# The last stage of a one-core PEER layer: groups of six expert tiles instead of four, with the sums taken in two halves

## The reference

```python
def block(args):
    xk, ik, gk = args
    act = jax.nn.gelu(jnp.einsum('tkd,td->tk', expert_u[ik], xk))
    return jnp.einsum('tk,tkd->td', gk * act, expert_v[ik])
...
x = x + peer_ffn(rmsnorm(x, norm2), peer_wq, peer_keys, peer_u, peer_v)
y_prompt = rmsnorm(xp, final_norm)
```

## Time and profile before

| what | value |
|---|---|
| median of 3 executions | 3219.15 us (3218.26 to 3221.4) |
| the profiled execution's own time | 3221.37 us |
| its span | 3219.6 us |
| mean granted TensorE clock | 0.987 of full speed |
| busy share of the span: PE, DVE, POOL | 97%, 80%, 35% |
| the last stage | from 2150 us to the end, a third of the span |
| HBM traffic | 233 GB/s over the span |

### The profile page before, as it was taken

One profiled execution on the slowest core, in us unless ns is written; L12 is line 12 of the kernel. 1 busy time (PEld: TensorE's weight loads), 2 busy tenths in 40 slices (PEclk: granted clock), 3 DMA queues, 4 the chain that ended last, 5 costly groups with the idle time before them and its releaser, 6 DMA issues. The chain is left out here.

```text
span 3219.6 us, 45871 instructions
## 1 busy us (share of the span) xinstructions
PE 3107.1 (97%) x17420; PEld 2726.2 (85%) x17420; DVE 2569.2 (80%) x5687; ACT 883.4 (27%) x1307; POOL 1126.0 (35%) x758
## 2 busy tenths in 40 slices
PE   8999989899999999999999999998999999999998
PEld 7867765499999999999999999987777777777776
DVE  6621244357799999989888988858999999999996
ACT  4210300132122222224444444422222222222222
POOL 0000000000032222223333333324555886688881
PEclk9999989999999999999999999999999999999999
DMA  3010021351187777768888889899999999999993
GB/s 103 15 41 29 14 88 51 99 163 55 49 264 246 246 243 245 243 209 287 294 286 325 288 292 325 285 331 339 343 344 343 336 347 350 339 344 346 347 347 138
DMA packets 359908, 754.88 MB, mean 234 GB/s; under 512 B 37085, under 2 KB 205881, under 8 KB 354041
## 3 DMA queue, kind: packets, MB, share of 16 engines
q0 software_dynamic: 102576, 373.47, 34.3%
q1 hardware_dynamic: 257112, 378.49, 34.0%
HBM read 647.21 MB, written 102.25 MB: 233 GB/s over the span
## 5 line engine op out<-in xcount | busy, mean ns | idle before, releaser
L1931 POOL DMA_INDIRECT lead<-in_peer_v_dram,chosen x212 | 424.2, 2001 | 179.1 <-DVE acc_s L1950 128.1
L1931 POOL DMA_INDIRECT gr_row<-in_peer_u_dram,chosen x205 | 229.8, 1121 | 462.0 <-DVE chosen L1940 454.5
L1907 ACT ACTIVATE up_a<-up_pa 128x352 f32<-128x352 f32 x256 | 118.9, 464 | 755.3 <-PE up_pa L1892 662.5
L1931 POOL DMA_INDIRECT dr_row<-in_peer_v_dram,chosen x140 | 282.6, 2019 | 99.9 <-DVE acc_s L1950 72.4
L2694 DVE TENSOR_TENSOR acc<-pd_po,acc 128x512 f32<-128x512 f32 x384 | 278.7, 726 | 25.5 <-PE pd_po L2761 22.6
L1931 POOL DMA_INDIRECT s_sb<-in_peer_u_dram,chosen x147 | 159.3, 1084 | 374.7 <-DVE chosen L1940 369.1
L1950 DVE SCALAR_TENSOR_TENSOR acc_s<-lead,chosen,acc_s 128x1024 f32<-128x1024 f32 x212 | 279.9, 1320 | 0.0
L2340 ACT ACTIVATE lo_wx<-room 128x704 fp32r<-128x704 f32 x128 | 101.6, 794 | 623.6 <-DVE room L2331 623.6
L1940 DVE CUSTOM_DVE_ANT_0 gr_row<-gr_row,xs 128x1024 f32<-128x1024 f32 x205 | 248.6, 1220 | 14.4 <-DMA gr_row<-in_peer_u_dram,chosen 14.4
L511 PE MATMUL fr_a<-pj_w,h_t 128*128 128x256 f32 (+1 forms) x864 | 199.3, 393 | 0.9 <-PEq L186 0.9
L2462 DVE TENSOR_SCALAR pg_hot_i<-pg_iota,sel_t 128x128 f32<-128x128 f32 x704 | 195.7, 358 | 0.0
(11 more groups left out here) (484 smaller groups left out, 7420.1 us busy)
## 6 DMA issues: line engine op xcount, KB each, us to landing
lead<-in_peer_u_dram SPq DMA_DIRECT2D x128, 512.0 KB
room<-in_peer_v_dram SPq DMA_DIRECT2D x128, 512.0 KB
act_d<-up_a SPq DMA_DIRECT2D x256, 176.0 KB
room<-w_d SPq DMA_DIRECT2D x64, 704.0 KB, 6.6
room<-act_d SPq DMA_DIRECT2D x64, 704.0 KB
w_d<-pg_wb SPq DMA_DIRECT2D x24, 1024.0 KB, 7.0
w_d<-room SPq DMA_DIRECT2D x20, 1024.0 KB
lead<-in_peer_wq_dram SPq DMA_DIRECT2D x20, 512.0 KB, 3.9
```

The lines of the kernel that those rows point to most:

```text
L1907: self.nc.scalar.activation(self.a_sb[c][:], self.pa[c][:, 0:WB], ACT.Gelu_apprx_tanh).then_inc(self.a_act, 1)
L1931: pool.indirect_dma_start(self.buf[i % self.n], None, self.table, bass.IndirectOffsetOnAxis(ap=self.idx[:, col:col + 1], axis=0)).then_inc ...
```

## The change

Groups of six tiles (`GE = 6`), the last of eight: `NG = 21`. The operands of eight tiles are one ring (`RING = 8`): tile m is written where tile m - 8 was, as soon as PE has used that tile for the last time (`freed`). PE makes a group's sums in two halves of six sums, and inside a half goes tile by tile over six PSUM banks at once. The two banks of the fold join the others, so eight go round (`NBANKS`), one half of the sums in six of them while two more are free. DVE's order is written anew in ticks (one tile of one half, 17 matmuls): 240 ticks and the last group's. The operands are made eight ticks ahead, by `made_by`. The rows are spread by `ROOM_AT` over the six ticks of a half: one, then two in each of four, then none. The additions of a half's sums stand together: four at the end of its last tick, two at the start of the next. Some loads of `acc` are issued later at the start, and slots leave in another order at the end.

```diff
-GE = 4
+GE = 6
+RING = 8
...
-        self.nc.scalar.activation(self.vx[m // GE % 2][m % GE][0], self.v[m % 2], ACT.Copy).then_inc(self.v_hi, 1)
+        self.nc.scalar.activation(self.vx[m % RING][0], self.v[m % 2], ACT.Copy).then_inc(self.v_hi, 1)
...
+SIZES = (GE,) * 20 + (NK - 20 * GE,)
+NG = len(SIZES)
 OUTS = 2 * ND
+HALF_OUTS = OUTS // 2
...
-FIRST_ROW = 12
-ROWS_EARLY = 18
...
+TICKS = 2 * GE * (NG - 1)
+AHEAD = 8
+ROWS_FROM, ROWS_TO = 6, TICKS - 4
+ROOM_AT = (1, 2, 2, 2, 2, 0)
+
+FINAL = (6, 7, 0, 1, 8, 2, 5, 3, 4)
...
+def made_by(tick):
+
+    return min(3 * NK, 3 * (tick + AHEAD) // 2 + max(0, 3 * (tick - TICKS + 6) // 2))
...
-                g, e = m // GE, m % GE
-                if e == 0 and g >= 2:
-                    act.wait_ge(o_done, OUTS * (g - 1))
+                if m >= RING:
+                    g, e = (m - RING) // GE, (m - RING) % GE
+                    if e < GE - 1:
+                        act.wait_ge(freed, (GE - 1) * g + e + 1)
+                    else:
+                        act.wait_ge(filled, sum_at(g, OUTS - 1) + 1)
...
-            for g in range(NG):
-                for o in range(OUTS):
-                    m = GE * (g + 1) + o // 3
-                    if g == 0:
-                        add(g, o)
-                    if m < NK:
-                        (lower.multiply, lower.low_v, lower.low_w)[o % 3](dve, m)
-                    if g >= 1:
-                        add(g, o)
-                    at = OUTS * g + o - FIRST_ROW
-                    for i in range(rows_by(at), rows_by(at + 1)):
...
+            for tick in range(TICKS + SIZES[-1]):
+                last = tick >= TICKS
+                g = NG - 1 if last else tick // (2 * GE)
+                half, e = (0, tick - TICKS) if last else divmod(tick % (2 * GE), GE)
+                if e == 0 and tick >= GE:
+                    for o in (HALF_OUTS - 2, HALF_OUTS - 1):
+                        add(g if half else g - 1, o + (0 if half else HALF_OUTS))
+                make(made_by(tick), made_by(tick + 1))
+                for i in range(rows_by(tick), rows_by(tick + 1)):
+                    if i == 0:
+                        dve.wait_ge(accs_in, 16 * NXS)
+                    rows_v.add(dve, i, gate, acc_s)
+                if e == SIZES[g] - 1:
+                    for o in range(HALF_OUTS - 2):
+                        add(g, HALF_OUTS * half + o)
...
+            def half_sums(g, half):
+                for e in range(SIZES[g]):
+                    m = GE * g + e
+                    if half == 0:
+                        pe.wait_ge(v_lo, m + 1)
+                        pe.wait_ge(w_lo, m + 1)
+                    for o in range(HALF_OUTS * half, HALF_OUTS * (half + 1)):
+                        if e == 0:
+                            bank_free(sum_at(g, o))
                         mm = product(g, o, e)
-                    mm.then_inc(o_done, 1)
+                        if e == SIZES[g] - 1:
+                            mm.then_inc(filled, 1)
+                    if half == 1 and e < SIZES[g] - 1:
+                        mm.then_inc(freed, 1)
```

More of the change, by code:

```diff
@@ new lines, in _ @@
+            g = NG - 1
+            inverse(0)
+            add(g, HALF_OUTS - 2)
+            inverse(1)
+            add(g, HALF_OUTS - 1)
+            take(FOLD_REST, x_s)
+            dve.wait_ge(gain_loaded, 16)
+            weigh(0)
+            inverse(2)
+            weigh(1)
+            add(g, HALF_OUTS)
+            inverse(3)
+            weigh(2)
+            add(g, HALF_OUTS + 1)
+            inverse(4)
+            weigh(3)
+            take(FOLD_HALF, acc[0:HALF_P, ND - 1, :])
+            inverse(5)
@@ L2755, in _ @@
+            weigh(4)
+            add(g, HALF_OUTS + 2)
+            inverse(6)
+            weigh(5)
+            add(g, HALF_OUTS + 3)
+            inverse(7)
+            weigh(6)
+            add(g, HALF_OUTS + 4)
+            weigh(7)
+            add(g, HALF_OUTS + 5)
+            inverse(8)
+            weigh(8)
         @block.tensor
@@ L2760, in product @@
                 for x, y in parts:
-                    mm = nc.tensor.matmul(po[(OUTS * g + o) % NPO][:], lower.tokens(wx[g % 2][e], s, y),
-                                          vx[g % 2][e][x][:, half * W4:(half + 1) * W4],
-                                          start=(e == 0 and (x, y) == parts[0]), stop=(e == GE - 1 and (x, y) == parts[-1]))
-                return mm
-            for e in range(GE):
-                pe.wait_ge(v_lo, e + 1)
-                pe.wait_ge(w_lo, e + 1)
-                for o in range(NPO):
-                    mm = product(0, o, e)
-                    if e == GE - 1:
-                        mm.then_inc(o_done, 1)
@@ new lines, in product, with bank_free @@
+                    mm = nc.tensor.matmul(banks[sum_at(g, o) % NBANKS][:], lower.tokens(wx[m % RING], s, y),
+                                          vx[m % RING][x][:, half * W4:(half + 1) * W4],
+                                          start=(e == 0 and (x, y) == parts[0]), stop=(e == SIZES[g] - 1 and (x, y) == parts[-1]))
+                return mm
+            def bank_free(at):
+                if at == NBANKS - 1:
+                    pe.wait_ge(up.a_act, 2 * NK)
+                if at >= NBANKS:
+                    pe.wait_ge(emptied, at - NBANKS + 1)
@@ new lines, in _ @@
+            for g in range(NG - 1):
+                for half in range(2):
+                    half_sums(g, half)
+            half_sums(NG - 1, 0)
+            pe.wait_ge(shaped, PACKED)
+            pe.wait_ge(rows_v.used, COLS)
+            fold_into(FOLD_REST, LAST, [(fold[i], acc_s[:, NSP + i, :]) for i in range(len(PACKS))])
+            for o in range(HALF_OUTS, OUTS):
+                if sum_at(NG - 1, o) == FOLD_HALF + 2:
+                    pe.wait_ge(emptied, BASE + 2)
+                    fold_into(FOLD_HALF, HALF_P, [(fold[0][:, 0:HALF_P], acc[:, ND - 1, :])])
+                bank_free(sum_at(NG - 1, o))
+                for e in range(SIZES[-1]):
+                    mm = product(NG - 1, o, e)
+                mm.then_inc(filled, 1)
```

144 lines of the change are left out of this document (57 added, 87 removed).

## The result

| kernel | median | runs | ratio to before, 95% interval |
|---|---|---|---|
| before | 3220.28 us | 4 (3218.26 to 3221.79) | |
| changed | 3247.99 us | 4 (3244.54 to 3252.86) | 1.0084 (1.0072 to 1.0097) |

The changed kernel is slower, by 28 us. I had forecast 102 us. Its profiled execution took 3246.93 us, its span is 3245.2.

A forecast was written before the change was run, and what follows sets the result against it. DVE bounds the stage. Its 12 ticks were put at 47.3 us plus 7.5 of row waits, D = 54.8; 2290.0 + 18.83 x D gave 3322 us, 3.2% slower, with an 8-in-10 range of 3212 to 3363.

The forecast's parts named there:

- the term for the port: Middle stage: POOL's fetches are held during DVE's two-operand SBUF work, so DVE waits 7.5 us for rows in 12 ticks.
- With that boundary open: If fetches can leave between an operand step and a row, DVE's row waits are 6.5, 7.9 and 6.4 us.
- Seven openings for 9.2 rows: Per half, three fetches leave during additions, four before pairs' second rows; two leave only because DVE has run dry.
- a fetch of 2901.42: Fetch in the kernel before, started during a row and ending 0.81 us after the low part behind it.
- The third rival: Part of the port's cost: step-into-row openings open, landings short, waits 2.1 to 5 us, 3220 to 3275 us; chance 16%.
- 47.3 us without waits: DVE's 12 ticks in the stage: additions, rows and operands 45.97 us plus 1.3 for second rows of pairs.
- D: Time of 12 ticks in the stage, forecast as 47.3 + 7.5 = 54.8 us.
- PE's pace: PE's matmuls in the stage at 0.2288 us each, 204 in 12 ticks: 46.7 us, nothing added for bank changes.
- The sum: Whole execution: 2290.0 + 18.83 x D, from the span of 3219.6 us; 3322 us with D at 54.8.
- PE runs free to its last sum: After tick 236 DVE has no rows, so PE is unhindered to the stage's end; 1.5 us less there.
- The loads bound: Rival: loads of 17.1 MB in 12 ticks take 48.5 us, 3203 us; 4%, within the 14% for an uncounted port.
- Signs: Expected profile: DVE idle 6 to 9 us per 12 ticks for rows, PE waiting about 4 us each half.

The follow-up runs named there:

- e2: Changed kernel with six row buffers in place of five, two packed acc_s slots merged into one and one small start load left out: 3208.69 us, ratio 0.9958.
- e3: Changed kernel with each row fetch bringing 256 KB, half the bytes, with as many descriptors: 3201.36 us, ratio 0.9939.
- e10: Changed kernel with rows brought by plain loads that SP issues through the hardware queue, POOL fetching nothing in this stage: 3202.34 us, ratio 0.9936.
- e7: Changed kernel with sparse columns reordered so a pair's two rows belong to two acc_s slots and the second doesn't wait: 3259.91 us, ratio 1.012.
- e5: Like e1 (operand steps and rows one by one), plus one VectorE wait per half behind the last addition of the run: 3174.84 us, ratio 0.9848.
- e9: Kernel before, with POOL's row transfers as plain DMAs of 128 neighbouring rows instead of indirect ones: 3224.16 us, one execution.
- e6: Kernel before, with one VectorE wait in each group of 12 sums, for the addition just issued: 3227.72 us, ratio 1.0017.
- e1: Changed kernel with VectorE's operand steps and rows one by one in each half, so rows no longer pair: 3204.43 us, ratio 0.9936.
- e4: Changed kernel with both steps and rows one by one and six row buffers: 3207.95 us, ratio 0.9951.

## Why the prediction was right or wrong

**The step that failed** is the term for the port: "With that boundary open the waits are 6.5, 7.9 and 6.4. The mean of the six is 7.5", and under it "Seven openings for 9.2 rows". It measured 2.8 us in 12 ticks. I took a fetch of 2901.42, held across row and low part, as the rule for that boundary. It belonged to a run of late fetches, in a stretch in which VectorE hadn't waited for 670 us. The changed kernel waits in every pair, and behind a row that VectorE has waited for, the boundary to the next step let out every fetch that asked, 111 of 111. I had counted the gap inside the pair as an opening, but not the one that it makes behind the pair. The third rival, "Openings that I count as shut (operand step into row) are open", gave 3220 to 3275 us for 16%, and holds 3248, but not by its own account: it named the boundary from a step into a row, where 37 fetches left, not that from a row to a step, and it counted on short landings, and these are not short: 6.35 us above, where I had stepped through 3.6, 4.5 and 5.5. That my range of 3212 to 3363 holds the time is luck as well. It reached down to the break-even, and its middle rests on the port. The 2.8 us of waits that are left come from five buffers against a trip of fetch and landing, as e2, e3 and e10 show; the port is in it with part of the fetch, and a port more shut makes them larger (68.2 us in 800 in e7).

**The other terms**, at their word:
- *47.3 us without waits* (45.97 and 1.3 for pairs). D less row waits is 50.2 - 2.8 = 47.4 in the changed kernel, 47.6 in e3 and e10 (47.8 less 0.2). Right. The pair: 2.67 us for two rows, thus 1.39 from start to start in place of 1.19, 0.20 for my 0.16.
- *PE's pace.* 0.2288 a matmul was 1% high: e5 makes 3,510 in 797 us, 0.2271. The more frequent bank changes cost nothing that shows.
- *Start.* Tile 8's multiply began at 2195.9, forecast 2195.5.
- *The sum.* 2290.0 + 18.83 x 50.2 = 3235.3 for a span of 3245.2. The 10 us that lack stand behind tick 234. PE waited 5.2 us for the last group's banks, since VectorE had waited for the loads of the last tiles (2.7 and 2.3 us), and its clock fell:

```profile
3137.00:3165.00 28.00, 25.93 (x106) 0.94 0.86 308
3165.00:3175.00 10.00, 5.40 (x15) 0.66 0.05 19
```

A share of 0.94 in 28 us is 1.7 us of full speed, 0.66 in 10 us is 3.4, part of it in the wait itself. "PE runs free to its last sum" was wrong by this much, and the clock that I left out is some of it.
- *The loads bound.* I gave 360 GB/s at a share of 1; e5 moved 366 at 0.99. By that the loads didn't bind even at 46.5 us in 12 ticks.
- *Signs.* Waits on `lead` and `dr_row`, PE's wait at the third sum: right. The sizes were too large: 28 waits of PE, 44.3 us together, for the 31 halves in 800 us, and 4.1 the longest, where I had put 4 in each. Fetches of 1 to 1.7 us amid rows and low parts, which I had named as the sign against the port step, were there (2722.29 and 2724.28).

The Trainium skill (SBUF — State Buffer, section "Who interferes with whom") infers that tensor_tensor doesn't delay a DMA, since descriptor making needs only the write side. By e9 that holds for a plain DMA that POOL issues, 0.53 us each; it doesn't for an indirect one, of which 197 took 2.29 us and more in before.

**Where the gain went.** The change takes 79 us of additions from VectorE, and without waits D would have been 46.5 to 47.4: faster than before, as e5 shows. It was given back by two rows to a tick with five buffers (45.0 us of waits in the middle, where before had none), by the pairs (160 x 0.20 = 32 us of VectorE's time), and by 10 us at the end.

## What to carry to other kernels

A measured stall has a condition. Before pricing it a hundred times over, look at what the engine did ahead of that one case, and at cases where it didn't happen: the 2.62 us of 2901.42 needed a row that VectorE hadn't waited for. A number that comes out as a theory said (e6) doesn't show the theory's reason; look at the single events too. When work is moved into clumps, work out the trip of a buffer (release, issue, landing) against the time in which the clump uses them all, beside the averages: here 9.2 us against the 8.2 that five buffers leave. And where VectorE works without a pause beside POOL's indirect fetches, a wait of 0.14 us now and then can be worth 30 us.

## What the runs showed that I had not expected

- VectorE's instructions start at fixed distances, but their busy times grow while it doesn't wait: rows from 1.28 to 1.36 us in before over 900 us, to 1.32 in e1 within 53 us. A wait of 0.04 us (e5) sets them back. With plain DMAs in place of indirect ones they reached 1.294. Why they grow was not settled.
- From a step to a row the overlap goes with whether an indirect fetch gets in between: free to 0.10 us, one half at 0.12, held from 0.13 (e1; in e4 28 free and 29 held at 0.12, 5 held at 0.13).
- From a row to a step it is the wait ahead of the row: 427 of 427 left behind a row that VectorE had waited for, 352 of 358 were held behind another, at overlaps of 0.08 as at 0.17. Why is not settled.
- POOL's fetches stay late once they are late. In before 2.76 us of POOL standing still were followed by 67 long fetches, and the second time by 130 to the end; in e6, with a pause in each group, by 7 to 10. Nobody waited for them in either kernel.
- A VectorE instruction that waits for the one just ahead starts 0.04 us after its end where the pause is (2380.81 to 2380.85); a pause costs 0.14 us in all, 45.81 for 45.53 us with two of them in 12 ticks.
- This core moved 366 GB/s over 800 us in e5, at a share of 0.99.
